# Opening of a hybrid encoder block: rows of block one in pairs, its products in halves of 256 tokens, four weight lists in place of three

## What is computed

```python
h = layer_norm(x, in_ln_g, in_ln_b)                       # (1, 2048, 1024)
proj = h @ w_in                                           # 1024 -> 1792
q, k, v, u = split(proj, [512, 640, 768])
a, gate = split(u, 2)                                     # 512 channels each
c = causal_depthwise_conv(a * sigmoid(gate), conv_w, conv_b)   # 31 taps
```

## Time and profile before

| what | before |
|---|---|
| median of 3 runs | 1901.06 us (1899.74 to 1901.9) |
| span of the profiled execution, first to last instruction | 1897.6 us |
| PE busy | 1859.7 us (98%), 8632 matmuls |
| DVE, ACT, POOL busy | 1515.5, 959.7, 894.1 us (80%, 51%, 47%) |
| mean granted TensorE clock | 0.997 of full speed |

### The profile page before, as it was taken

How to read it: one execution, slowest core, us unless ns; L and a number is a source line. 1 busy time by engine, 2 the same in 40 slices (tenths; PEclk the granted TensorE clock), 3 DMA queues, 4 the chain that set the end, 5 groups by cost and what they waited for, 6 DMA issues and landing times.

```text
span 1897.6 us, 27021 instructions
## 1 busy us (share of the span) xinstructions
PE 1859.7 (98%) x8632; PEld 1526.1 (80%) x8632; DVE 1515.5 (80%) x1926; ACT 959.7 (51%) x1503; POOL 894.1 (47%) x666
## 2 busy tenths in 40 slices
PE   8999999999999799999999999999999999999998
PEld 7788888777777688888888778888888788888886
DVE  8777994799998887888888988878787755776787
ACT  4555662777778544444445544444444432232453
POOL 2169994266675354345445544444442875430000
PEclk9999999999999999999999999999999999999999
DMA  7411123644563423333334333232324644587554
GB/s 279 175 44 44 44 83 123 207 132 142 172 207 116 144 106 130 130 116 105 122 138 172 118 116 111 99 111 94 106 104 157 189 153 142 163 265 246 183 170 145
DMA packets 201829, 265.80 MB, mean 140 GB/s; under 512 B 12320, under 2 KB 131360, under 8 KB 200480
## 3 DMA queue, kind: packets, MB, share of 16 engines
q1 hardware_dynamic: 188096, 229.32, 36.7%
q10 hardware_dynamic: 13664, 35.66, 5.1%
HBM read 177.18 MB, written 87.75 MB: 140 GB/s over the span
## 4 chain that ended last, share of the span: by engine, by line
PE 72%; DVE 11%; issue 5%; ACT 4%; DMA 4%; POOL 3%; SPq 1%; DVEq 0%; POOLq 0%; ACTq 0%
PE u_mm L2408 35%; PE d_y L2837 21%; PE a_mm L254 14%; DMA u_w_raw<-w_up 2%; ACT m_ce L1781 1%; PE m_y L2457 1%; ACT m_tps L1773 1%; DVE m_stat L2192 1%; DVE m_top L2236 1%; DVE m_den L2249 1%; DVE u_forms L1962 1%; DVE u_w_lo L1953 1%; PE a_acc L658 1%; DMA d_wd_raw<-w_down 1%; ACT m_probT L1828 1%
## 5 line engine op out<-in xcount | busy, mean ns | idle before, releaser
L2408 PE MATMUL u_mm<-u_forms,u_w_hi 128*128 128x512 f32 x2464 | 761.1, 390 | 8.7 <-DVE u_forms L1962 3.4
L2408 PEld LDWEIGHTS u_mm<-u_forms,u_w_hi 128*128 128x128 f32 x2464 | 462.2, 188 | 108.8 <-issue 11.0
L2408 PE MATMUL u_mm<-u_forms,u_w_lo 128*128 128x512 f32 x1232 | 479.9, 390 | 0.0
L2837 PE MATMUL d_y<-d_wd,d_a_hi 128*128 128x512 f32 x1232 | 379.4, 389 | 2.6 <-DVE d_a_lo L1054 2.0
L254 PE MATMUL a_mm<-a_hT,a_w_hi 128*128 128x512 f32 x896 | 278.1, 392 | 1.5 <-DVE a_hT L557 1.5
L2837 PEld LDWEIGHTS d_y<-d_wd,d_a_hi 128*128 128x128 f32 x1232 | 231.1, 188 | 51.3 <-DVE d_a_lo L1054 2.4
L2408 PEld LDWEIGHTS u_mm<-u_forms,u_w_lo 128*128 128x128 f32 x1232 | 231.5, 188 | 48.2
L2837 PE MATMUL d_y<-d_wd,d_a_lo 128*128 128x512 f32 x616 | 239.6, 389 | 0.0
L1993 DVE SCALAR_TENSOR_TENSOR u_y<-u_z,u_taps,u_y 128x1024 f32<-128x1024 f32 x176 | 222.6, 1287 | 10.4 <-DVE u_z L2007 3.2
L254 PEld LDWEIGHTS a_mm<-a_hT,a_w_hi 128*128 128x128 f32 x896 | 166.7, 188 | 37.0 <-DVE a_hT L557 3.0
L1363 POOL TENSOR_TENSOR u_w_sum<-u_w_raw 128x512 f32<-128x512 f32 x44 | 59.4, 1349 | 263.9 <-DMA u_w_raw<-w_up 258.2
(11 more groups left out here) (250 smaller groups left out, 2944.8 us busy)
## 6 DMA issues: line engine op xcount, KB each, us to landing
u_w_raw<-w_up SPq DMA_DIRECT2D x44, 1024.0 KB, 5.2
d_a_raw<-gated_scr SPq DMA_DIRECT2D x56, 704.0 KB, 5.3
gated_scr<-u_s SPq DMA_DIRECT2D x88, 256.0 KB, 2.0
d_wd_raw<-w_down SPq DMA_DIRECT2D x88, 256.0 KB, 5.2
gated_scr<-u_gy SPq DMA_DIRECT2D x44, 256.0 KB, 2.2
a_xs<-x SPq DMA_DIRECT2D x16, 512.0 KB, 5.7
m_h_in<-h_scr SPq DMA_DIRECT2D x16, 512.0 KB, 3.9
h_scr<-m_r SPq DMA_DIRECT2D x16, 512.0 KB, 4.7
```

The source lines that it names most:

```text
L2408: last = nc.tensor.matmul(mm[BANK[s]][:], w[:, s, k, :], forms[:, POS[s], part, k, :], start=(s in FRESH and k == 0 and w is w_hi and part ...
L2837: m = nc.tensor.matmul(dy[u % BANKS][:], a[:, u % 2, k, :], wd[:, ph % 2, k, part, :], start=(k == 0 and a is a_hi and part == HI_PART), s ...
```

## The change

Seven things change, all in the first stage:

1. SP loads rows 0 and 1 first, then the norm's gain and bias, list 0, rows 2 and 3, lists 1 and 2; list 3 once list 0's low part is made, and the first reloads behind it. ACT issues the identity's load.
2. In block one DVE makes the moments, the root and the result of rows 0 and 1 first, then those of rows 2 and 3. All four rows are finished on DVE (no `norm_last` or `shift_last`). ACT takes the moments of row 2 there.
3. In blocks two to four ACT takes the moments of two rows (0 and 1), DVE those of rows 2 and 3.
4. `OPEN = 4`: a1 joins the opening, with tiles `a_w3_*`, `a_w4_*` of its own. DVE makes the low parts of lists 2 and 3.
5. Block one is multiplied with four lists in two halves of 256 tokens (`half_sweeps`), 32 steps each; the first half needs rows 0 and 1 only. Blocks two to four have three lists (`sweeps`), and the fourth list of these blocks comes after them. The places of the transposes are `FIRST`, `SECOND`, `THIRD`.
6. The convolution's products and sums for group 0 start in the opening (`tap_products`, `tap_sums`), and both borders are zeroed at the start (`pad_ok` is gone).
7. The build call passes `dynamic_dma_scratch_size=512`, which makes room for the tiles.

The core of the diff:

```diff
-OPEN = 3
+OPEN = 4
-        BY_ACT, BY_DVE = 1, (0, 2, 3)
+        ACT_ROWS, DVE_ROWS = ((2,), (0, 1), (0, 1), (0, 1)), ((0, 1, 3), (2, 3), (2, 3), (2, 3))
+        def opened(n, i):
+            if n == 0:
+                return i
+            return OPEN + 3 * (n - 1) + i if i < 3 else OPEN * (NB - 1) + n
@@ SP
-            for i in range(OPEN):
-                load_list(i)
+            first_row(0)
+            first_row(1)
+            sp.dma_start(g_bc, row_to_all(ln_g)).then_inc(g_ld, 16)
+            sp.dma_start(b_bc, row_to_all(ln_b)).then_inc(b_ld, 16)
+            load_list(0)
+            first_row(2)
+            first_row(3)
+            load_list(1)
+            load_list(2)
+            sp.wait_ge(wlo_ok, 1)
+            load_list(3)
+            reload(0, 0)
@@ ACT, block two to block four
+            take_root(3, 0, RB)
+            nc.scalar.preload_act_table(ACT.Sigmoid)
+            norm_last(1)
+            open_a(0)
+            open_gate(0)
+            hi_of(1, 0)
+            open_q(0)
+            hi_of(1, 1)
+            open_next(0)
+            moments(2, 0)
+            hi_of(1, 2)
+            moments(2, 1)
+            hi_of(1, 3)
+            take_root(4, 0, RB)
...
+            hi_of(2, 3)
+            open_q(1)
+            moments(3, 0)
+            moments(3, 1)
+            take_root(5, 0, RB)
+            norm_last(3)
@@ POOL
+            pool.wait_ge(h_ok, 2)
+            weights_lo(0)
+            weights_lo(1)
-            pool.wait_ge(mm_ok, OPEN * NB)
-            nc.gpsimd.memset(glu[:, 1, :, 0:LEAD], 0.0).then_inc(pad_ok, 1)
@@ DVE, from block one's second pair on
+            roots(2, HALF_ROWS, RB)
+            scale(0, 2)
+            shift(0, 2)
+            weights_lo(2)
+            weights_lo(3)
+            scale(0, 3)
+            shift(0, 3)
+            lo_of(0, 2)
+            stats(1, 2)
+            lo_of(0, 3)
+            stats(1, 3)
+            block_stats(1)
+            scale(1, 0)
+            shift(1, 0)
+            scale(1, 1)
+            shift(1, 1)
+            lo_of(1, 0)
+            scale(1, 2)
+            lo_of(1, 1)
+            shift(1, 2)
+            scale(1, 3)
+            lo_of(1, 2)
+            stats(2, 2)
+            lo_of(1, 3)
@@ PE
+            FOUR, THREE = 4 * KT, 3 * KT
+            FIRST = ((0, 2, 12), (0, 3, 25), (1, 0, FOUR + 18), (1, 1, FOUR + 23))
+            SECOND = ((2, 0, 10), (2, 1, 14), (2, 2, 16), (2, 3, 21))
+            THIRD = ((3, 0, 11), (3, 1, 14), (3, 2, 16), (3, 3, 19))
+            with pe.Fori(0, 6) as _:
+                keep_busy(8)
+            half_sweeps(0, 4, done, 2 * FOUR)
+            transposes(1, 2)
+            transposes(1, 3)
```

More of the change, by code:

```diff
@@ L302, in weights_hi, with take_root, moments @@
                 nc.scalar.copy(list_hi(i), list_raw(i)).then_inc(whi_ok, 1)
[L304 to L316, removed]
+            def take_root(count, first, last):
+                act.wait_ge(veps_ok, count)
+                nc.scalar.activation(root[:, first:last], veps[:, first:last], ACT.Sqrt).then_inc(root_ok, 1)
+            def moments(n, r):
+                done = moments_before(n) + 3 * ACT_ROWS[n].index(r)
+                act.wait_ge(x_ld[r], 16 * n + 16)
+                if done:
+                    act.wait_ge(moment_ok, done)
+                nc.scalar.activation(spare[:, 0:D], xs[:, r, :], ACT.Identity, scale=1 / D, accum_out=mv[:, r, 0:1]).then_inc(moment_ok, 1)
+                act.wait_ge(moment_ok, done + 1)
+                nc.scalar.activation(mean_part[:], mv[:, r, 0:1], ACT.Copy, scale=1 / 32).then_inc(moment_ok, 1)
+                act.wait_ge(moment_ok, done + 2)
+                nc.scalar.activation(spare[:, 0:D], xs[:, r, :], ACT.Square, bias=mean_part[:], scale=-1 / 32,
+                                     accum_out=mv[:, r, 1:2]).then_inc(moment_ok, 1)
             def norm_last(n):
                 r = RB - 1
[L320 to L322 removed]
+                act.wait_ge(nmr_ok, n)
+                act.wait_ge(h_st[r], 16 * n)
                 nc.scalar.activation(row(n, r), xs[:, r, :], ACT.Identity, bias=nmr[:, r:r + 1],
@@ new lines, in _ @@
+            norm_last(3)
+            open_a(2)
+            hi_of(3, 0)
+            open_gate(2)
+            hi_of(3, 1)
+            hi_of(3, 2)
+            hi_of(3, 3)
+            open_q(2)
+            open_a(3)
+            open_gate(3)
+            weights_hi(4)
+            open_q(3)
+            tap_products(0, 0)
+            for n in range(1, NB):
+                open_next(n)
+                if n == 1:
+                    weights_hi(5)
+                tap_products(0, n)
+            act.wait_ge(half_pi_ok, 1)
@@ new lines, in _ @@
+            act.wait_ge(ang_ok, 2)
+            nc.scalar.activation(trig[:, 0, :], turns[:], ACT.Sin, bias=half_pi[:], scale=-1.0).then_inc(trig_ok, 1)
+            nc.scalar.activation(trig[:, 1, :], ang[:], ACT.Sin).then_inc(trig_ok, 1)
+            nc.scalar.activation(trig[:, 2, :], ang[:], ACT.Sin, scale=-1.0).then_inc(trig_ok, 1)
+            act.wait_ge(trig_ok, 3)
+            act.dma_start(trig_scr.rearrange("c f (t q) -> (f t) c q", t=NT), trig[:, :, :]).then_inc(trig_st, 16)
+            for r in range(RB):
+                act.wait_ge(h_st[r], 16 * NB)
@@ L659, in transposes, with half_sweeps @@
                 last.then_inc(tp_ok, 1)
+            def half_sweeps(n, count, first, last):
+                for at in range(first, last):
+                    half, step = divmod(at, count * KT)
+                    i, k = divmod(step, KT)
+                    e = opened(n, i)
+                    if step == 0:
+                        pe.wait_ge(lo_ok, RB * n + 2 * half + 2)
+                    if half == 0 and k == 0:
+                        if n == 0:
+                            pe.wait_ge(wlo_ok, i + 1)
+                        else:
+                            pe.wait_ge(mm_free, e - NB + 1)
+                    m = product(list_hi(i), list_lo(i), n, k, e % NB, slice(half * (BLK // 2), (half + 1) * (BLK // 2)))
+                    if half == 1 and k == KT - 1:
+                        m.then_inc(mm_ok, 1)
             def sweeps(n, first, last):
```

289 lines of the change are left out of this document (163 added, 126 removed).

## The result

The changed kernel takes 1908.6 us (median of 6 runs, 1907.6 to 1911.65), the one before 1901.5 in the same series: a ratio of 1.0041, 95% interval 1.0030 to 1.0052. It is slower by 7 to 8 us, and the interval leaves out a ratio of 1. The profiled execution has a span of 1905.6 us against 1897.6, so +8.0.

The account below looks back on a forecast made before the run. The prediction took TensorE (PE) as the bound, its opening products moving all that follows. Terms from -8.9 for the earlier start to added waits summed to +7.8, plus 1.6 for the clock: 1901.06 + 7.8 + 1.6 = 1910.5 us, range 1902 to 1915.5.

Parts of the forecast that it names:

- Start of useful work: Block one's first useful product on PE starts at 18.2 in place of 27.05: -8.9 us.
- Halves: Block one's 96 products of 512 columns become 192 of 256, at 0.125 us each: +2.2 us.
- Row 2 of block one: New PE wait: DVE's small variance operation is held beside POOL's low part, row ready at 23.8, wanted at 22.7: +1.2 us.
- Block two's last rows: PE waits 1.7, 2.8 and 3.1 for block two's last two rows and low part, products start at 56.0: +7.6 us.
- Block four's first row: ACT makes two rows' moments behind q, so the row is ready 12.1 after block three's start, PE at 7.5: +4.7 us.
- The clock: TensorE's clock falls to 1.2 GHz after a long wait; one fall counted in full: +1.6 us.
- the rival with repeated falls: The clock falls at every long wait, two to three times, costing 3.3 to 5.0 us: 1914 us, chance 0.18.
- The convolution's start: Convolution no longer waits for its border but needs block four's gate, about 114; costs nothing, DVE not on the chain.
- The rest moves along: After the opening, everything waits in turn on PE or its products; nothing later is tied to the launch.
- +1.7 (turns): Rows 2 and 3 of block one are transposed after the start and no longer before it, 0.85 each: +1.7 us.
- the old waits' 2.0: Four short PE waits for a row or its low part in the old opening go away: -2.0 us.
- The rival "faster": Rows 1 to 3 of block two keep up with PE; wins once waits total under 7.0 us; 1896.1 us, chance 0.12.

Follow-up runs that it names:

- whole_block: Changed kernel with block one multiplied whole, in 512 columns after its fourth row, identity products before it: 1922.0 us, ratio 1.0096 to the kernel before.
- filled_waits: Changed kernel with identity products in TensorE's waits around block two's last two transposes and ahead of block four's first: 1904.4 us, ratio 1.0025 to the kernel before.
- scalar_order: Changed kernel with only ScalarE's operations reordered as in reordered; VectorE's order and TensorE's steps unchanged: 1902.7 us, ratio 1.0003 to the kernel before.
- reordered: Changed kernel, same operations with ScalarE's order, VectorE's order and the steps of TensorE's transposes moved: 1896.4 us, ratio 0.9972 to the kernel before.
- reordered_early: reordered with the first list's high parts multiplied first, orders and steps moved again, variance sum as a two-input operation: 1896.7 us, ratio 0.9974 to the kernel before.
- late_row: Changed kernel with block four's rows transposed behind steps 18, 20, 22, 24 instead of 11, 14, 16, 19: 1906.5 us, ratio 1.0031 to the kernel before.

## Why the prediction was right

The forecast was 1910.5 us, 9.4 over the kernel before, with slower at 0.78; measured were 1908.6, 7.1 over. It was right by its mechanism, and its terms came out so:

- **Start of useful work, -8.9.** Measured -8.25 (18.80). VectorE's copies ended 0.6 later than placed; the chain was the one described.
- **Halves, +2.2.** Measured +1.2: 192 products at 0.119 to 0.120 are 23.0 us against 21.8. The old row of 0.1275 with weights of 64 columns was too dear. The 0.109 of the Trainium skill ("TensorE: Matmul & The Clock Gate", Back-to-back issue gap), an estimate from its formula, is too cheap for this stream. And whole_block shows that the price is a tenth of what the halves bring.
- **Row 2 of block one, +1.2.** Measured 1.05, and by the cause named: VectorE's 1.96 us beside GpSimd's 2.38 (18.22 to 20.60).
- **Block two's last rows, +7.6** (1.7, 2.8 and 3.1). Measured 1.71, 2.48 and 2.36, together 6.55; its products start at 56.35, placed at 56.0.
- **Block four's first row, +4.7.** Measured 4.65. The 0.8 for its third row did not come: TensorE was slow just then and not early. In filled_waits, where it was not slow, 0.51 of it came (at 94.71).
- **Block three's start, +0.5.** Measured 0.31.
- **The clock, +1.6, is the term that was mis-sized.** It fell twice and cost about 4.8 us in the first execution and 3.8 in the second by the rows, and 3 to 4 by filled_waits. "One fall that costs in full" counted the products behind one wait; the second wait of 4.65 us alone was longer than the 3.41 that had sufficed before, and each fall also stretched the transposes ahead of it, which delays the row's copy. On this term the rival with repeated falls was nearer, though its total of 1914 was not.
- **The convolution's start** was placed at 114, when block four's gate comes; it began at 119.53, with the gate's product by GpSimd done at 119.1. It is 12 us later than before and still not on the chain.
- **"The rest moves along"** can't be judged from one execution. The opening came to +10.9 and +9.8 in two executions (9.4 forecast), the whole to +8.0 and +10.3 by the spans and to +7.1 and +8.2 by the medians. Part of the gap is the fast execution of before; where the rest goes is not shown. The opening was forecast too low and the total too high: the near hit of the total owes something to luck.

With -8.25, +1.2, +1.7 (turns), +1.05, +6.55, +4.65, +0.31, -2.0 and the clock's 4.8 the sum is +10.0. But the old waits' 2.0 are counted between starts of products, and the new ones as idle time, which is 0.2 or so less for each; their idle time before is 1.4. Counted between starts, as the old ones, the six new waits come to 13.7 and not 12.6 (1.21, 1.87, 2.75, 2.62, 0.47 and 4.81, without what the clock adds). With that the sum is +11.2, where block four's products show 11.1, so nothing of size is left over up to there.

Of the signs named, block two's products began at 56.35 and not before 51, and TensorE stood before block four's first row; the last product of a1 came at 138.7, just outside the 136 to 138 given, in step with the opening's 11.1 in place of 9.4.

The rival "faster" named the right point: with the waits below 7.0 together the change would win. scalar_order has 7.0 us of waits and a ratio of 1.0003, a match that is partly luck, as it also has a fall of the clock, which that rival leaves out; reordered has 2.6 and wins 4 to 5 us, where the sum for that rival gave 1896.1 and 1896.4 was measured.

## What to carry to other kernels

Work that is started earlier pays only as far as what it runs into is earlier too: list what each later row or tile needs, in the order of the engine that makes it, and move that order first (here ScalarE's, worth 7 us), the consumer's second (6 us more, and nothing by itself). Put long independent preparations, such as a next block's moments, ahead of operations that wait for TensorE, since behind them they inherit that wait. And price a wait on TensorE with the clock that it may cost: here 12.6 us of waits cost some 3 to 5 us more, and products of the identity in the waits, at no cost of their own, gave that back. The length of one wait did not tell whether the clock falls: behind 2.42 us in reordered_early it fell, behind 2.36 us in late_row (at 103.75) it stayed at 1.00. And the same waits cost 1 us more or less from one execution to the next.

## What the runs showed of the hardware

GpSimd and VectorE exclude one another, in both directions and only for some operations. In the changed kernel VectorE's small operation that started at 18.67 stood 1.96 us, to GpSimd's end at 20.60, where 0.17 is usual, and at 119.53 a tensor_tensor of 1.24 us took 3.03, beside GpSimd's from 119.07 to 121.47. The other way round, in reordered, GpSimd's row operation of 2.37 us took 3.34, as it began while VectorE was in one of 1.28 us that ran from 44.19 to 45.47:

```profile
44.35 3.34 POOL L533 TENSOR_TENSOR a_h_rows<-a_h_rows,a_gb 128x1024 f32<-128x1024 f32 x1 [23.48 <-DVE a_h_rows L628]
```

But VectorE's subtraction from PSUM passes: in the same kernel's VectorE timeline it took its usual 1.22 us in the midst of that,

```profile
45.39 1.22 DVE L647 TENSOR_TENSOR a_hT<-a_acc,a_hT 128x1024 fp32r<-128x1024 f32 x1
```

and so did the statistics of a row, 0.68 us from 14.78 in reordered_early, while GpSimd ran from 14.34 to 16.72. In these cases the one that starts second is the one that stands, even with two elements a row.
